# A hybrid decoder step on one core: order of VectorE's products, of the masked values and of the output norm's sums in the mixer

## What is computed

```python
q = _l2norm(q) * (DN_DK ** -0.5); k = _l2norm(k)
kb = k * beta; vb = v * beta
L = where(strict, (kb @ k.T) * decay, 0); A = L + I
u, w = solve(A, [vb, kb * exp(g)])
attn = where(tri, (q @ k.T) * decay, 0)
v_new = u - w @ S
o = (q * exp(g)) @ S + attn @ v_new
S = S * exp(g_last) + (k * exp(g_last - g)).T @ v_new
```

## Time and profile before

| | us |
|---|---|
| three runs | 4346.82, 4364.22, 4369.38 |
| their median | 4364.22 |
| span of the profiled execution, first to last instruction | 4329.5 |
| own time of the profiled execution | not given by the page |
| mixer's full turns, 486 to 1265 us | about 130 each |

### The profile page before, as it was taken

How to read it: one execution, slowest core, us unless ns; L and a number is a source line. 1 busy time by engine, 2 the same in 40 slices (tenths; PEclk the granted TensorE clock), 3 DMA queues, 4 the chain that set the end, 5 groups by cost and what they waited for, 6 DMA issues and landing times. The chain is left out here.

```text
span 4329.5 us, 66268 instructions
## 1 busy us (share of the span) xinstructions
PE 3728.3 (86%) x24298; PEld 3467.2 (80%) x24298; DVE 3020.4 (70%) x4791; ACT 1466.9 (34%) x1882; POOL 2050.1 (47%) x1144
## 2 busy tenths in 40 slices
PE   6786998999897898997678989899998888889986
PEld 3336888988886797997568888888988888888986
DVE  5777645455545224798977777777778788888886
ACT  5665343434443113222332332332332322232232
POOL 2343222222223233334046776677676667677672
PEclk9997999999998898998999999999999999999998
DMA  8981222222223122222489999999999999999994
GB/s 310 346 335 52 83 81 83 74 71 70 64 79 103 52 99 102 82 74 92 169 326 382 401 405 384 378 405 407 398 397 376 389 393 405 399 405 414 410 407 172
DMA packets 253137, 1090.68 MB, mean 252 GB/s; under 512 B 25353, under 2 KB 78857, under 8 KB 172297
## 3 DMA queue, kind: packets, MB, share of 16 engines
q1 hardware_dynamic: 167440, 543.60, 34.1%
q0 software_dynamic: 73728, 536.90, 30.4%
q10 hardware_dynamic: 11776, 7.52, 0.6%
HBM read 1047.54 MB, written 40.40 MB: 251 GB/s over the span
## 5 line engine op out<-in xcount | busy, mean ns | idle before, releaser
L248 POOL TENSOR_TENSOR wlo<-raw,whi 128x1024 fp32r<-128x1024 f32 x551 | 1342.6, 2440 | 1436.7 <-ACT whi L244 1431.0
L244 ACT CAST whi<-raw 128x1024 fp32r<-128x1024 f32 x670 | 697.2, 1049 | 1241.4 <-DMA raw<-in_u 554.8
L263 PE MATMUL gps<-hi_d,whi 128*128 128x320 f32 x2048 | 661.1, 323 | 126.4 <-POOL wlo L248 69.4
L2095 PE MATMUL gps<-chi,whi 128*128 128x320 f32 x2048 | 655.7, 320 | 111.6 <-DVE outacc L2224 83.8
L263 PE MATMUL gps<-lo_d,whi 128*128 128x320 f32 x2048 | 651.2, 318 | 0.0
L263 PE MATMUL gps<-hi_d,wlo 128*128 128x320 f32 x2048 | 650.4, 318 | 0.0
L2095 PE MATMUL gps<-clo,whi 128*128 128x320 f32 x2048 | 644.4, 315 | 0.0
L2095 PE MATMUL gps<-chi,wlo 128*128 128x320 f32 x2048 | 644.3, 315 | 0.0
L2182 DVE SCALAR_TENSOR_TENSOR dps<-ring,coef,dps 128x2048 f32<-128x2048 f32 x252 | 591.9, 2349 | 4.3 <-DVE dps L2182 0.5
L2169 DVE CUSTOM_DVE_ANT_0 ring<-ring,dps 128x2048 f32<-128x2048 f32 x256 | 582.3, 2279 | 0.0
L263 PEld LDWEIGHTS gps<-hi_d,whi 128*128 128x128 f32 x2048 | 401.6, 196 | 146.7 <-POOL wlo L248 78.6
(11 more groups left out here) (384 smaller groups left out, 5947.0 us busy)
## 6 DMA issues: line engine op xcount, KB each, us to landing
raw<-in_u SPq DMA_DIRECT2D x256, 512.0 KB, 9.5
raw<-in_v SPq DMA_DIRECT2D x256, 512.0 KB, 7.9
wada<-in_w_ada SPq DMA_DIRECT2D x96, 1024.0 KB, 6.3
raw<-in_w_in SPq DMA_DIRECT2D x96, 512.0 KB, 3.5
gateD<-gst SPq DMA_DIRECT2D x8, 2560.0 KB, 7.6
gate<-gateD SPq DMA_DIRECT2D x32, 640.0 KB, 17.1
raw<-in_w_out SPq DMA_DIRECT2D x32, 512.0 KB, 3.8
raw<-in_w_q SPq DMA_DIRECT2D x32, 512.0 KB, 4.0
```

Of the source, the lines that this page charges most:

```text
L244: act.copy(whi[:, k.slot, :], raw_of(k)).then_inc(W.hi, 1)
L248: pool.tensor_tensor(wlo[:, k.slot, :], raw_of(k), whi[:, k.slot, :].bitcast(F32), ALU.subtract).then_inc(W.lo, 1)
L263: m = pe.matmul(gps[:, bank, 0:DT], w, x[:, kt, :], start=(kt == 0 and n == 0), stop=(kt == KT - 1 and n == 2))
L2095: m = pe.matmul(gps[:, 2 + dt, 0:DT], w[:, slot, cols], x[:, buf, c, :], start=(c == 0 and n == 0), stop=(c == NG - 1 and n == 2))
```

## The change

Four things change in the mixer. DVE makes kgd right after kb and sets S.prod there; nkeg, qg, nkq and v follow, and v sets a new semaphore S.prod2, on which PE waits ahead of L919 and SP ahead of the row load. On DVE vn and vmask stand ahead of the LRU step in slot 23. The second half of the LRU step (hlast, gy) moves to slot 25, behind the level update of slot 24, and conv(0) from slot 25 to 26. PE's sums of the output norm move from slot 46 to 47. The count of chained steps falls by one, as S.prod and S.prod2 are waited for directly.

```diff
 NSP = 2 * NST * H * TOPK
 PACK = 5 * CW + 4 * NB * PL + 2 * P + NB
 ACT_STEPS_A_TURN = 27
-DVE_STEPS_A_TURN = 81
+DVE_STEPS_A_TURN = 80
 LOW = -3.0e38
 AHEAD = 2
 NBANK = 512
...
             S.ocp, S.osq, S.onrm, S.oinv, S.oout = sems(c3, "p3_ocp", "p3_osq", "p3_onrm", "p3_oinv", "p3_oout")
             S.sload, S.stcl, S.o_out, S.st_out, S.sst_out = \
                 sems(c3, "p3_sload", "p3_stcl", "p3_o_out", "p3_st_out", "p3_sst_out")
-            S.conv_out, = sems(c3, "p3_conv_out")
-            spent_outs = range(S.mix.num, S.conv_out.num + 1)
+            S.conv_out, S.prod2 = sems(c3, "p3_conv_out", "p3_prod2")
+            spent_outs = range(S.mix.num, S.prod2.num + 1)
             NL = LEVELS - 1
             SLOTS = 48
 
...
                                 sp.dma_start(row(mixD, h), gy[:, :]).then_inc(S.lrust, 16)
                                 sp.dma_start(row(a["lru_h_t"], h), hlast[:, :]).then_inc(S.lrust, 16)
                                 if B:
-                                    sp.wait_ge(S.prod, g + 1)
+                                    sp.wait_ge(S.prod2, g + 1)
                                 r = rowsD[h:h + 1] if isinstance(h, int) else rowsD[bass.ds(h, 1)]
                                 sp.dma_start(rows[:, :, :].rearrange("p r t -> p (r t)"),
                                              r.rearrange("h r t -> h (r t)").broadcast_to([P, 4 * T])
...
 
                                 pe.wait_ge(S.sload, g * 16 + 16)
                                 pe.wait_ge(S.tcop, g + 1)
+                                pe.wait_ge(S.prod2, g + 1)
                                 for b in range(NB):
                                     m = pe.matmul(dps[:, 3, 192 + b * 16:192 + (b + 1) * 16], sst[:, b, :],
                                                   nkq[:, b, :, :], start=True, stop=True)
...
                                         pe.wait_ge(S.sup0, g + 1)
                                     pe.matmul(dps[:, 3, :], ktok[0:TS, NCH, :], vmask[0:TS, n * 4:n * 4 + 4, :],
                                               start=True, stop=True).then_inc((S.dss0, S.dss1)[n], 1)
-                            if e == 46 and B:
+                            if e == 47 and B:
                                 pe.wait_ge(S.osq, g + 1)
                                 pe.wait_ge(S.sup, g * NCH + NCH)
                                 for th in range(2):
...
                                 ch(tt(kc, kc, sqs[:, 1, :], ALU.mult))
                                 ch(stt(qc, qc, float(P) ** -0.5, sqs[:, 0, :], ALU.mult, ALU.mult))
                                 ch(tt(kb[:, :], kc, rows[:, 1, :], ALU.mult))
-                                ch(tt(vc, vc, rows[:, 1, :], ALU.mult))
+                                tt(kgd[:, :], kc, rows[:, 3, :], ALU.mult).then_inc(S.prod, 1)
+                                dve.wait_ge(S.prod, g + 1)
                                 ch(stt(nkeg[:, :], kb[:, :], -1.0, eg, ALU.mult, ALU.mult))
                                 ch(tt(qg[:, :], qc, eg, ALU.mult))
                                 ch(dve.tensor_copy(nkq[:, :, 0, :], samples(nkeg)))
                                 ch(dve.tensor_copy(nkq[:, :, 1, :], samples(qg)))
-                                tt(kgd[:, :], kc, rows[:, 3, :], ALU.mult).then_inc(S.prod, 1)
-                                dve.wait_ge(S.prod, g + 1)
+                                tt(vc, vc, rows[:, 1, :], ALU.mult).then_inc(S.prod2, 1)
+                                dve.wait_ge(S.prod2, g + 1)
                                 dve.wait_ge(S.st_out, g * 16 + 16)
                                 dve.memset(st[:, :], 0.0).then_inc(S.stcl, 1)
                                 dve.wait_ge(S.stcl, g + 1)
...
                                 ch(dve.tensor_copy(samples(kb), x[:, :, 1, :]))
                                 tt(rst[:, 0:TS].rearrange("p (b s) -> p b s", b=NB), x[:, :, 0, :], samples(vc),
                                    ALU.add).then_inc(S.rts, 1)
+                            if e == 23 and B:
+                                dve.wait_ge(S.vsm, g + 1)
+                                ch(dve.tensor_copy(vn[0:TS, 1, :], dps[0:TS, 3, 192:320]))
+                                tt(vmask[0:TS, :, :], bc(vn[0:TS, 1, :].unsqueeze(1), [TS, NB, P]),
+                                   bc(const[0:TS, C_BM:C_BM + NB].unsqueeze(2), [TS, NB, P]), ALU.mult).then_inc(S.vms, 1)
+                                dve.wait_ge(S.vms, g + 1)
                             if e == 23 and A:
                                 dve.wait_ge(S.sqrt, h + 1)
                                 dve.wait_ge(S.sigi, h + 1)
...
                                 dve.tensor_tensor_scan(ry[:, c], la[:, c], iu[:, c], 0.0, ALU.mult,
                                                        ALU.add).then_inc(S.scan, 1)
                                 dve.wait_ge(S.scan, h + 1)
+                            if e == 25 and A:
                                 if later:
                                     dve.wait_ge(S.lrust, h * 32)
                                 ch(dve.tensor_copy(hlast[:, 0:1], ry[:, TP - 1:TP]))
...
                                 ch(tt(gy[:, 0:TP], gy[:, 0:TP], ry[:, 0:TP], ALU.mult))
                                 tt(samples(gy), samples(gy), padded(ry, 0, NS), ALU.mult).then_inc(S.lruout, 1)
                                 dve.wait_ge(S.lruout, h + 1)
-                            if e == 23 and B:
-                                dve.wait_ge(S.vsm, g + 1)
-                                ch(dve.tensor_copy(vn[0:TS, 1, :], dps[0:TS, 3, 192:320]))
-                                tt(vmask[0:TS, :, :], bc(vn[0:TS, 1, :].unsqueeze(1), [TS, NB, P]),
-                                   bc(const[0:TS, C_BM:C_BM + NB].unsqueeze(2), [TS, NB, P]), ALU.mult).then_inc(S.vms, 1)
-                                dve.wait_ge(S.vms, g + 1)
                             if e == 26 and B:
                                 dve.wait_ge(S.ats, g + 1)
                                 tt(kb[:, TP:T], kb[:, TP:T], dps[:, 3, 448:512], ALU.add).then_inc(S.oss, 1)
...
                                     dve.wait_ge((S.dss0, S.dss1)[n], g + 1)
                                     tt(v, v, dps[:, 3, :].rearrange("p (b v) -> p b v", v=P),
                                        ALU.add).then_inc((S.sup0, S.sup1)[n], 1)
-                            if e == 25 and A:
+                            if e == 26 and A:
                                 conv(0, 1, e2, S.evq, S.cvq)
                             if e == 34 and A:
                                 conv(1, 0, em, S.evk, S.cvk)
```

## The result

| | before | after |
|---|---|---|
| median of the runs, us | 4366.80 (4346.82 to 4383.52, 4 runs) | 4305.86 (4298.31 to 4309.29, 4 runs) |
| span of the profiled execution | 4329.5 | 4305.7 |
| its own time | not given | 4307.65 |
| seven full turns, first to last start of DVE's k product | 907.4 (129.63 a turn) | 862.7 (123.24 a turn) |
| last turn, last k product to DVE's first step on the mixer's transposed output | 102.0 | 98.9 |

The account below looks back on a forecast made before the run. PE sets the pace in full turns, standing still 60.8 us in all at the Gram products and L961. 7 x (2.84 + 2.24) - 4.35 + 1.75 = 33.0 us off 4364.2 gives 4331 us, range 4305 to 4350.

Parts of the forecast that it names:

- one of the signs that the prediction named for its being wrong: At the change of turns: the forecast would be wrong if L885 or L896 waited longer for ACT; no size given.
- part 3: Output norm's sums one slot later: ACT's chain starts 1.6 us later, 4.35 us lost over the kernel where uncovered.
- Rival A: Conv(0) not held by POOL, or POOL's cast falls beside it: 44.6 us won, 4320 us; chance 0.18.
- Part 1's term: At the Gram products: with kgd earlier, S.prod comes 2.84 us earlier per full turn, leaving PE a 2.43 us wait.
- I leave the cost as it is: Behind the Gram wait: the lower clock's cost taken as unchanged; ends 1.4 won, 0.3 lost.
- 1.4 won: Behind the Gram wait: the favourable end for the clock's cost, 1.4 us; the other end was 0.3 lost.
- Part 2's term: Masked values ahead of the LRU step, second half and conv(0) later: 2.24 us won per turn, not 3.41.
- my sum of DVE's steps: DVE's steps after the level update, conv(0) held by POOL, put L994's start at 809.8 instead of 812.09.
- Rival B: ACT's chain at the change of turns has no cover: 9.6 us lost there, 27.7 won, 4336 us; chance 0.14.
- The last turn: No GEMM beside the chain: 3.35 us won before L1242, chain in front starts 1.6 later, +1.75 us net.
- Rival C: New short waits at L932 and L994 bring the lower clock: 11.9 us less, 21.1 won, 4343 us; chance 0.18.
- Rival D: Slower: shorter, closer waits at the Gram products, L932 and L994 keep PE at the lower clock, 4401 us; chance 0.05.

Follow-up runs that it names:

- the run with the later cast: The changed kernel with ACT's weight cast of slot 28 moved to slot 30: ratio to before 0.986, mixer 1035.1 us.
- the second execution: The changed kernel, unaltered, run and profiled once more: ratio to before 0.9893, mixer 1041.9 us.
- part 1 alone: The kernel before with only kgd and S.prod moved ahead of nkeg, qg, nkq and v: ratio 0.9944, mixer 1060.3 us.
- both casts moved: Slot 4's cast to slot 0, slot 28's to 30: changed kernel 0.984, mixer 1018.8 us; with sums back in slot 46, 0.9823, 1009.8 us.
- parts 1 and 2: The changed kernel with the output norm's sums back in slot 46: ratio to before 0.9884, mixer 1035.9 us.

## Why the prediction was right, and where it was off

**The sign and the mechanism** hold step by step: kgd took over vc's 2.79 us, the Gram wait became 2.44 per turn for a forecast of 2.43, L961 waits no longer, L932 waits 0.60 (0.6 to 1.1 forecast) and L994 0.29 (about 0.5), POOL holds one of conv(0)'s multiply-adds, and ACT's idle time ahead of its logarithm is gone in five of six changes of turn. But one of the signs that the prediction named for its being wrong did come: L885 waited longer for ACT, 5.8 us in six changes of turn for 0.8 in one before. That is what the prediction's own part 3 leads to, as ACT's squares come a slot later: the sign did not fit the sum. Rival A is excluded by the 4.63, and the run with the later cast shows that the hold matters. By the rule of the Trainium skill that the prediction quotes, "SBUF — State Buffer", section "Who interferes with whom", conv(0) was to be held; the trace agrees, 4.63 us for three that take 2.60 undisturbed.

**Part 1's term** (2.84 per turn) was exact: 14.12 for 16.96. What failed is the sentence on the clock behind the Gram wait, "I leave the cost as it is". The stretch from L896 to L912 became 8.1 us shorter in seven turns (5.9 in the second execution, 3.8 with part 1 alone). Its end "1.4 won" per turn was in the range, but I took the middle.

**Part 2's term** (2.24 per turn) was too small; alone, the part wins 23.3 us in seven turns, 3.3 each, 3.2 of them between L912 and the second L994. I had it from one turn, the one in the earlier trace rows. In that turn L961 to the first L994 took 7.99 us; in three of the seven it was 9.01 to 9.05, because the low clock behind the 3.4 us wait lasted longer there (6.8 us for 3.4). In the turn that I read, L912 to the second L994 goes from 56.3 to 53.5, 2.75; in those three, 3.8. That is the plainest mistake: a cost that includes the clock has to be read over all turns. The other 0.5 lies in my sum of DVE's steps, which has the second L994 that much too late.

**Part 3's term** (4.35, and 1.6 at the last turn's start, 5.95 together up to the last k product) cannot be told from right with one execution of each kernel: over that stretch, part 3 costs 4.2 us alone, 5.1 or 8.2 in the whole change by which of its two executions is taken, and 8.2 with both casts moved. I gave the uncovered part of ACT's delay in full to S.prod. PE's slot moved out of the way at the same time, and the low clock behind the restart's pause, which two of the six changes of turn had before (12.6 to 12.7 us from L1000 to L885 instead of 10.0 to 11.0), did not come in the first execution after (10.0 each) and came once in the second. Rival B (9.6 lost, and 1.6 at the last turn) lies above all of these.

**The last turn** came out as forecast: its L885 waits 8.6 us for ACT instead of 7.0, the 1.6 of the sum, and behind its k product it is 3.1 us shorter (3.35 forecast). That the second comes so near is partly luck, for the same stretch took 98.9 and 99.0 us in the two executions of this kernel and 102.1 with the cast of slot 28 moved, which does not touch it.

**The sum.** Forecast 33.0: part 1 with the last turn 19.9 + 3.35, part 2 15.7, part 3 -5.95. Measured alone: 27.2, 23.9 and -3.6. Of the 15.6 us between 33.0 and 48.6, 8.1 are the stretch behind the Gram wait and 6.5 the stretches from L912 to the second L994, of which 3.1 are the three turns with the longer low clock ahead of L994; 1 us is left, most of it in the first turn, which the change does not touch. By the second execution it is 12.6 us, 5.9 of them behind the Gram wait. So the mechanism was right, and what was mis-sized is the lower clock behind both of PE's waits, the one taken as unchanged and the other read from one turn, and next to it the sum of DVE's steps (3.4). Rival C (new short waits bring the lower clock) is excluded for waits of 0.3 to 1.1 us: in the profile after, the stretch behind each at L933, L995 and L912 was at full clock. Rival D did not come near.

**What stays open** is which of the turns fall to the lower clock behind a 2.4 us wait. One, three, four, four and six of seven were seen in five executions, with nearly the same wait. The sequence of instructions ahead of it is the same in each turn, so it is not this kernel's order alone that decides. No run here tries it. The same holds for the pauses at the loop's restart. The mixer of one kernel differs by 3 us between its two executions, and the clock is at least a part of that.

## What to carry to other kernels

Where POOL and DVE share the work of a loop, look for the DVE instructions that are longer in every turn than others of their shape, and see which POOL run they stand beside: moving the producer of that run (ACT's casts here, one four slots earlier and one two later) was worth 26 us on top of the 52 of parts 1 and 2. When a chain on DVE is reordered, list what stands behind each moved step and who waits for it: conv(0) ahead of a 0.22 us addition cost PE a wait of up to 1.6 us in six of seven turns. And price a wait of PE with the clock behind it, over all turns and not one. Last, what is held by POOL moves when its neighbours do: after every change, look again for which instruction has the long time.

## What was not expected of the hardware

- A copy of 128 x 8 elements, bare 0.17 us, took 2.10 in every turn beside a POOL run of 2.37 (2.085 to 2.114 in all eight), and the scan behind it was then free, 1.41 in all eight. Before, the copy was held once in eight, and in the other seven the scan took the wait in its place. In those seven the copy had started 0.08 to 0.14 us ahead of POOL's run; after, it started 0.29 to 0.87 us behind it. In the first turn with both casts moved no POOL run was near, and both were free: 0.17 and 1.41.
- The hold works both ways: POOL's run took 2.85 us when a product had started 0.17 us ahead of it.
- After the same wait of 2.44 us the clock was 1.00 in one turn and 0.50 in another of the same execution, and at 0.50 L912 came 0.9 us later (parts 1 and 2, without 3).
